# Stick-breaking weights: the exponential written back into its accumulation bank, hi and lo parts made from there

## The reference

```python
mask = k_pos[None, :] < q_pos[:, None]
z = einsum('bqhd,bkhd->bhqk', q, k) * scale
sp = where(mask, softplus(z), 0.0)
tail = cumsum(sp, axis=3, reverse=True) - sp
w = where(mask, exp(log_sigmoid(z) - tail), 0.0)
out = einsum('bhqk,bkhd->bqhd', w.astype(v.dtype), v)
```

## Time and profile before

| | before |
|---|---|
| median of 3 runs | 1479.47 us |
| lowest, highest | 1476.62, 1480.8 us |
| the profiled execution | 1480.7 us |
| its span, first to last instruction | 1478.9 us |
| PE busy | 1401.1 us (95%) |
| DVE busy | 659.8 us (45%) |
| ACT busy | 572.4 us (39%) |
| POOL busy | 549.3 us (37%) |
| mean granted TensorE clock | 0.962 |

### The profile page before, as it was taken

How to read it: one execution, slowest core, us unless ns; L and a number is a source line. 1 busy time by engine, 2 the same in 40 slices (tenths; PEclk the granted TensorE clock), 3 DMA queues, 4 the chain that set the end, 5 groups by cost and what they waited for, 6 DMA issues and landing times.

```text
span 1478.9 us, 17999 instructions
## 1 busy us (share of the span) xinstructions
PE 1401.1 (95%) x6564; PEld 1135.6 (77%) x6564; DVE 659.8 (45%) x1168; ACT 572.4 (39%) x959; POOL 549.3 (37%) x249
## 2 busy tenths in 40 slices
PE   6979888999899999999997999999899999999999
PEld 4767777887678888888886877777678888888887
DVE  5476676566542220122244888888633221022210
ACT  4233344454533221222333777666543322122220
POOL 5222221332454444344463211212174444344451
PEclk9978887888999999999999999999999999999999
DMA  5111010010222232222321111111032333223340
GB/s 203 57 43 44 28 33 12 24 33 1 68 100 95 90 123 80 84 99 88 128 80 61 58 43 43 46 53 44 28 100 86 100 99 115 71 86 99 104 131 36
DMA packets 29718, 107.73 MB, mean 73 GB/s; under 512 B 3424, under 2 KB 3680, under 8 KB 29664
## 3 DMA queue, kind: packets, MB, share of 16 engines
q1 hardware_dynamic: 29520, 106.97, 21.9%
q10 hardware_dynamic: 144, 0.02, 0.0%
HBM read 104.88 MB, written 2.10 MB: 72 GB/s over the span
## 4 chain that ended last, share of the span: by engine, by line
PE 69%; DVE 11%; issue 10%; ACT 8%; POOL 2%; DMA 0%; ACTq 0%; DVEq 0%; POOLq 0%
PE bank L290 19%; PE bank L286 19%; PE bank L287 19%; DVE cs_hi L1073 3%; POOL w_lo L274 2%; PE bank L638 2%; PE bank L368 1%; DVE cs_lo L1075 1%; ACT ca L1032 1%; ACT w_hi L262 1%; PE bank L433 1%; ACT ca L1030 1%; PE bank L723 1%; DVE h_lo L383 1%; PE bank L895 1%
## 5 line engine op out<-in xcount | busy, mean ns | idle before, releaser
L274 POOL TENSOR_TENSOR w_lo<-wraw,w_hi 128x1024 fp32r<-128x1024 f32 (+2 forms) x176 | 451.0, 2563 | 723.5 <-ACT w_hi L262 723.4
L286 PE MATMUL bank<-h_hi,w_hi 128*128 128x512 f32 x1024 | 414.8, 405 | 17.6 <-DVE h_lo L383 11.6
L287 PE MATMUL bank<-h_lo,w_hi 128*128 128x512 f32 x1024 | 408.8, 399 | 0.0
L262 ACT ACTIVATE w_hi<-wraw 128x1024 fp32r<-128x1024 f32 (+2 forms) x176 | 194.0, 1102 | 262.9 <-DVE x L606 171.4
L290 PE MATMUL bank<-h_hi,w_lo 128*128 128x512 f32 x1024 | 260.4, 396 | 0.0
L286 PEld LDWEIGHTS bank<-h_hi,w_hi 128*128 128x128 f32 x1024 | 196.2, 192 | 69.7 <-DVE h_lo L383 17.9
L287 PEld LDWEIGHTS bank<-h_lo,w_hi 128*128 128x128 f32 x1024 | 196.1, 192 | 44.3 <-issue 1.0
L290 PEld LDWEIGHTS bank<-h_hi,w_lo 128*128 128x128 f32 x1024 | 194.0, 189 | 45.5
L287 PE MATMUL bank<-f_lo,w_hi 128*128 128x512 f32 x352 | 138.9, 395 | 0.0
L286 PE MATMUL bank<-f_hi,w_hi 128*128 128x512 f32 x352 | 138.9, 395 | 0.0
L592 DVE TENSOR_TENSOR fu<-bank,rstd 128x512 f32<-128x512 f32 x44 | 30.4, 691 | 203.9 <-PE bank L290 203.9
(11 more groups left out here) (222 smaller groups left out, 2014.6 us busy)
## 6 DMA issues: line engine op xcount, KB each, us to landing
wraw<-in_w_in SPq DMA_DIRECT2D x141, 512.0 KB, 3.3
wraw<-in_w_down SPq DMA_DIRECT2D x32, 704.0 KB, 4.1
bwraw<-in_w_b SPq DMA_DIRECT2D x6, 416.0 KB, 3.2
x<-in_xt SPq DMA_DIRECT2D x8, 256.0 KB, 5.1
out<-x SPq DMA_DIRECT2D x8, 256.0 KB, 2.2
wraw<-in_w_in SPq DMA_DIRECT2D x3, 256.0 KB, 4.2
tabb<-in_tabs_b SPq DMA_DIRECT2D x1, 512.0 KB, 8.4
taba<-in_tabs_a SPq DMA_DIRECT2D x1, 512.0 KB, 9.1
```

Source lines behind the costliest of these rows:

```text
L262: nc.scalar.activation(whi[:, s, 0:width], wraw[:, s, 0:width], ACT.Copy).then_inc(S("w_hi"), 1)
L274: nc.gpsimd.tensor_tensor(wlo[:, s, 0:width], wraw[:, s, 0:width], whi[:, s, 0:width], ALU.subtract).then_inc(S("w_lo"), 1)
L286: nc.tensor.matmul(out_bank, w, src_hi[kt], start=(kt == 0), stop=False)
L287: nc.tensor.matmul(out_bank, w, src_lo[kt], start=False, stop=False)
```

## The change

The exponential `c_w_act` writes its result in place, into the bank that it reads, and no longer into `ca[j]`. `c_w_dve` takes both its hi copy and the minuend of its lo subtract from that bank. Semaphores, their counts and the order of all instructions stay; no instruction is added or removed, and `ca` still serves the softplus chain.

```diff
     def c_w_act(act, u, j, b):
         act.wait_ge(S(f"c_tail{j}"), u * 3 + (b + 1))
-        a = ca[j][:, BO[b]:BO[b] + BW[b]]
-        nc.scalar.activation(a, bank[ZB[j][b]][:, 0:BW[b]], ACT.Exp).then_inc(S(f"c_w{j}"), 1)
+        z = bank[ZB[j][b]][:, 0:BW[b]]
+        nc.scalar.activation(z, z, ACT.Exp).then_inc(S(f"c_w{j}"), 1)
 
     def c_w_dve(dve, u, j, b):
+        w = bank[ZB[j][b]][:, 0:BW[b]]
         r = slice(BO[b], BO[b] + BW[b])
         n = u * 3 + (b + 1)
         dve.wait_ge(S(f"c_w{j}"), n)
         if b == 0:
             dve.wait_ge(S(f"c_tail{j}"), u * 3 + 3)
-        nc.vector.tensor_copy(cshi[j][:, r], ca[j][:, r]).then_inc(S(f"c_whi{j}"), 1)
+        nc.vector.tensor_copy(cshi[j][:, r], w).then_inc(S(f"c_whi{j}"), 1)
         dve.wait_ge(S(f"c_whi{j}"), n)
-        nc.vector.tensor_tensor(cslo[j][:, r], ca[j][:, r], cshi[j][:, r], ALU.subtract).then_inc(S(f"c_wlo{j}"), 1)
+        nc.vector.tensor_tensor(cslo[j][:, r], w, cshi[j][:, r], ALU.subtract).then_inc(S(f"c_wlo{j}"), 1)
```

## The result

| | before | after |
|---|---|---|
| median of 6 runs | 1480.13 us | 1467.42 us |
| lowest, highest | 1474.0, 1482.22 | 1465.58, 1469.4 |
| ratio, 95% interval | | 0.9917 (0.9904 to 0.9930) |
| profiled execution, its span | 1480.7, 1478.9 | 1467.24, 1465.4 |
| DVE busy | 659.8 | 645.9 |

The change makes the kernel 12.7 us faster by the medians (10.4 to 14.2 by the ratio's interval) and 13.5 us by the profiled executions; 13.25 us were forecast.

What follows compares the result with a forecast made beforehand. The ScalarE and VectorE loop, with SBUF casts stalled behind GpSimd, was taken to set the pair. Six steady pairs x 2.04 + 1.01 = 13.25 us; 1479.47 - 13.25 = 1466.2 us, 8-in-10 range 1462.0 to 1472.0.

Steps and rivals of the forecast that it cites:

- What bounds the kernel, and the stall: Value stage: loop over ScalarE and VectorE sets the 32.39 us pair; 14 SBUF casts wait for GpSimd's w_lo, 2.25 and 2.12 us.
- without a break: ScalarE, from the pair's third w_hi at 907.90 us: works with no gap up to the next pair's weights.
- The exponential into its bank: L1065 on ScalarE, writing its bank: no difference; bounds 0.1 us shorter or twice as long, +0.6 us on 512 columns.
- rival of a slow exponential: L1065 slower by 0.6 us at two places of a pair: saves only 5.4 us, 1474.1 us; chance 0.08.
- The hi copy: L1073 reading the bank: 0.69 us on 512 columns, 0.55 on 384, without waiting for GpSimd.
- rival in which the stall stays: Bank-reading hi copy still waits for GpSimd: 1.78 us more per pair, 12.5 us slower, 1491.9 us; chance 0.07.
- The lo subtract: L1075 taking bank and cshi instead of ca and cshi: 0.69 us as now, no effect.
- The steady pair: First head -1.09 us, second head -0.95 us: the pair goes from 32.39 to 30.35 us.
- The ends: First pair saves 1.01 us, 0.06 from its first stall and 0.95 from its second; last pair 0.
- The last pair's cover: Last pair: dearer copies, +0.74 us by a head's third lo, hidden since TensorE takes it at 1063.79; otherwise at most 2 x 0.74.
- TensorE's limit: TensorE's pair limit is 32.39 - 2.7 = 29.7 us, so after the change it still waits about 0.7 us a pair.
- more than forecast: Faster exponential or cheaper copies until TensorE closes all gaps: pair 29.7 us, 17.2 us saved, 1462.3 us; chance 0.07.

Runs made afterwards that it cites:

- e1: Kernel before, with GpSimd making the lo part of only 8 of 1024 weight columns in the stick-breaking stage (stale data): 1455.94 us, ratio 0.9839.
- e4: Changed kernel with a second exponential into ca; hi copy reads ca in SBUF, lo subtract reads the bank: 1481.74 us, ratio 1.0009 to the kernel before.
- e5: Changed kernel with one more exponential per bank, first into ca, which nothing reads: 1475.93 us, ratio 0.9972 to the kernel before.
- e8: Changed kernel with one more VectorE copy of bank 1 (384 columns) among the first head's splits: 1469.61 us, ratio 0.9932 to the kernel before.
- e3: Changed kernel with a second exponential into ca; hi copy reads the bank, lo subtract reads ca and cshi in SBUF: 1481.12 us, ratio 1.0012 to before.
- e7: Changed kernel with each head's weight exponentials ahead of the w_hi of a weight chunk on ScalarE: 1457.96 us, ratio 0.9858 to the kernel before.
- e9: Kernel before (weights through SBUF) with each head's exponentials ahead of the w_hi of a weight chunk: 1473.70 us, ratio 0.9966.
- e6: Changed kernel keeping in banks only weights whose copy would meet GpSimd, the others copied from SBUF: 1460.84 us, ratio 0.9877 to the kernel before.

## Why the prediction was right, and where it was not

**What bounds the kernel, and the stall.** Right. The cast waited for GpSimd (e1), up to its end (e4), and the loop over ScalarE and VectorE set the pair one for one (e5, e8). The stall of the very first cast was longer than the rows of a middle pair say, 2.52 us, because there GpSimd had itself been held up (last section). ScalarE's stretch "without a break" from 907.90 us has one gap, 0.20 us before L1484 for VectorE's `co`; it lies on the same loop and changes no term.

**The exponential into its bank.** Taken at no difference. Measured are 577 ns on 512 columns and 477 on 384, against 598 and 490 with the output in SBUF: 0.01 to 0.02 us shorter, far inside the bounds of the sum. The rival of a slow exponential falls.

**The hi copy.** Forecast 0.69 and 0.55 us, measured 0.685 and 0.546, and no stall inside `w_lo`. The rival in which the stall stays falls. The Trainium skill (VectorE: DVE Perf Modes, Why PSUM operands drop a tier) has a bank operand keep an fp32 copy out of the faster mode, and the changed kernel's trace agrees: 685 ns from the bank, 427 ns for the copy of the same shape from SBUF (`cs_hi<-cs`, L1044). Taken alone that speaks against the change; here the faster copy was the one that had to wait.

**The lo subtract.** "Nothing" was right for the duration and missed a point: left with two SBUF inputs it would have stalled in its turn (e3). The change needed both lines.

**The steady pair.** First head: from the cast to `cyk` 5.43 us before, 894.09 - 889.78 = 4.31 after, -1.12 (forecast -1.09). Second head: to `cyv`, 902.15 - 898.44 = 3.71 after, 0.98 less by the same rows of before, -0.95 forecast. Pair 30.27 against 30.35.

**The ends.** By the second marker the rows give -1.69 - 0.62 = -2.31 us, and -2.55 if the 0.24 us are taken out by which the execution after was behind when the stage began. The forecast there is 1.01 for the first pair and 1.56 for the second's first stall, 2.57. As forecast, next to nothing of the first pair's first stall is left by its second head, whose first copy starts at 837.96 - 0.24 = 837.72 against 837.74 us. The last pair's cover held.

**TensorE's limit was the step that failed.** "TensorE is the limit: 32.39 - 2.7 = 29.7 us" and, from it, "it still waits about 0.7 us". The limit is 28.91 (e1, e7), and the wait that remained is 1.3 us by the weight-load row, which fits 30.27 - 28.91 = 1.36. I had added up one row of the wait view, the four waits for `cs_lo`. A fifth wait of the same line stands in another row, under "issue", as the view names no releaser for it. Before, the row from the same view as the earlier trace rows, and TensorE's timeline where it waited:

```profile
PEld bank L1087 <- issue: 1.1, 1, 1.1
```

```profile
905.41 0.47 PE L1087 MATMUL bank<-cs_hi,cv 128*128 128x512 f32 x1 [0.69 <-DVE cs_lo L1075]
```

It is the load of the second head's first value matmul, at 905.38 us. The matmul itself stands in the timeline as waiting for `cs_lo L1075`, whose first part ends at 904.57 + 0.69 = 905.26 us. With it the weight loads of a pair waited 2.7 + 1.1 = 3.8 us, where the waits cost 32.39 - 28.91 = 3.48. So the row of four was too little by a wait, and all five together are a little too much. Stretches show it better: before, the first head's value matmuls ran from 896.38 to 898.65, 2.27 us; without a wait they take 1.16 to 1.17, which makes 1.10 us for this head and leaves 2.38 for the second. The changed kernel's, then the second head's wait:

```profile
893.54 0.39 PE L1088 MATMUL bank<-cs_hi,cv 128*128 128x512 f32 x1
...
894.71 0.28 PE L1088 MATMUL bank<-cs_lo,cv 128*64 128x256 f32 x1
...
902.29 0.38 PE L1088 MATMUL bank<-cs_hi,cv 128*128 128x256 f32 x1 [0.70 <-DVE cs_lo L1076]
```

And with the exponentials first:

```profile
891.52 0.39 PE L1088 MATMUL bank<-cs_hi,cv 128*128 128x512 f32 x1
...
892.68 0.28 PE L1088 MATMUL bank<-cs_lo,cv 128*64 128x256 f32 x1
```

The wrong limit did no harm to the forecast, since it was not reached. It put the floor of the rival "more than forecast" (1462.3 us) about 5 us too high (0.79 us in each pair), and the expectations of e1 and e7, which used 29.5, some 3 to 4 us.

**The size.** 13.5 us in the profiled executions, 12.7 by the medians, 13.25 forecast. The measured 1467.42 lies 1.2 us above the predicted 1466.2; half of that is the kernel before, whose median was 1479.47 us in the forecast and 1480.13 beside the changed kernel.

## What to carry to other kernels

When a VectorE copy shows a maximum far above its median, lay GpSimd's timeline beside it: if it ends a fixed bit behind a GpSimd instruction, the cure is one SBUF input fewer, and a bank can be the source although the copy then runs at 0.69 instead of 0.42 us. Apply it only where the two meet, and check each neighbour with two SBUF inputs, for the stall passes to the next one. Take the limit of the engine next in line from its gapless stretches, start to start, and not from one row of its waits: the waits of one line can stand in several rows.

## What the runs showed of the hardware

- A VectorE copy from SBUF to SBUF issued during a GpSimd subtract ended 0.27 to 0.29 us behind it, whether issued 0.06 or 0.9 us after its start (e9, e4). A VectorE subtract of two SBUF tiles ended 0.54 us behind it on 512 columns (e3) and 0.41 us on 384 (e9: 892.03 + 2.65 = 894.68, `w_lo` ends 894.27). GpSimd took its 2.39 to 2.42 us all the same.
- Where GpSimd came second, it was GpSimd that waited. In the first pair VectorE makes two lo parts of q from two SBUF tiles each. In the changed kernel `w_lo` was issued 0.72 us behind the start of the first, when the second was running, and took 2.95 us:

```profile
826.52 1.39 DVE L1125 TENSOR_TENSOR cq_lo<-cyq,cq_hi 64x512 fp32r<-64x512 f32 x2
```

```profile
827.24 2.95 POOL L274 TENSOR_TENSOR w_lo<-wraw,w_hi 128x1024 fp32r<-128x1024 f32 x1 [11.99 <-ACT w_hi L262]
```

  The kernel before shows the same (2.94 us). In e3, e4, e5, e6 and e8 `w_lo` was issued 0.63 to 0.67 us behind the start and took 2.40 or 2.41 us, and VectorE's two took 3.58 to 3.62 us instead of 1.39. So less than 0.1 us decided which engine stood still for the rest of the other's instruction; what this does to the time of the whole kernel is not shown.
- The remainder behind GpSimd's end is 0.13 to 0.15 us shorter than the instruction alone: 0.27 to 0.29 us for the copy that takes 0.42, 0.54 for the subtract that takes 0.69, 0.41 for the one that takes 0.56.
- Two bank-reading copies with no wait between them start 0.46 us apart at 0.55 us each (e8).
- Equal code ahead of the stage came out up to 6 us apart between profiled executions (790.44 to 796.43 us to the same instruction), more than several effects here: stretches between markers can be compared where spans can't.
